# Last two output pairs by token halves, and what follows them: a two-block model kernel on one Trainium2 core

## The reference

```python
y = concat([hyena_out, attn_out]) @ w_out_2          # 2048 x 2048
x = x + rmsnorm(y, post_mix_gain_2)                  # mean square over the 2048 channels of a token
z = rmsnorm(x, pre_ffn_gain_2)
gu = z @ w_up_2                                      # then a 3-tap convolution, gelu(gate) * up
x = x + rmsnorm(h @ w_down_2, post_ffn_gain_2)       # the output
```

## Time and profile before

| | us |
|---|---|
| device time, median of 3 runs | 2695.18 (2695.12 to 2695.7) |
| profiled execution, device time | 2694.55 |
| its span, first to last instruction | 2692.7 |
| PE busy in it | 2670.3 |

### The profile page before, as it was taken

How to read it: one execution, slowest core, us unless ns; L and a number is a source line. 1 busy time by engine, 2 the same in 40 slices (tenths; PEclk the granted TensorE clock), 3 DMA queues, 4 the chain that set the end, 5 groups by cost and what they waited for, 6 DMA issues and landing times.

```text
span 2692.7 us, 40238 instructions
## 1 busy us (share of the span) xinstructions
PE 2670.3 (99%) x14726; PEld 2327.2 (86%) x14726; DVE 1733.7 (64%) x1908; ACT 1279.2 (48%) x1354; POOL 23.0 (1%) x39
## 2 busy tenths in 40 slices
PE   8999999999999999999999999999999999999998
PEld 7888888888888888888888888888888888888887
DVE  7646566667767555555555667778677764577755
ACT  6444444444445444434444555545554443444443
POOL 0000000000011000000000000000000000000000
PEclk9999999999999999999999999999999999999999
DMA  6555455455555555565555555443545555555553
GB/s 237 198 188 172 172 187 180 165 185 188 189 174 198 187 187 198 172 206 191 187 189 171 183 201 173 165 146 130 214 146 190 190 206 196 194 188 187 187 189 139
DMA packets 74948, 494.44 MB, mean 184 GB/s; under 512 B 8711, under 2 KB 9640, under 8 KB 22072
## 3 DMA queue, kind: packets, MB, share of 16 engines
q1 hardware_dynamic: 74728, 493.41, 53.2%
q10 hardware_dynamic: 144, 0.01, 0.0%
HBM read 491.29 MB, written 2.10 MB: 183 GB/s over the span
## 4 chain that ended last, share of the span: by engine, by line
PE 96%; DVE 1%; ACT 1%; issue 1%; DMA 0%; SPq 0%; DVEq 0%; ACTq 0%
PE acc L1851 50%; PE acc L1859 26%; PE acc L1904 7%; PE acc L1910 4%; PE acc L1979 2%; PE acc L1984 1%; ACT w_hi L607 1%; PE acc L2117 1%; PE aux L2199 1%; PE aux L2264 1%; DVE w_lo L1093 0%; DMA raw<-in_w_in 0%; PE aux L2011 0%; PE acc L2124 0%; PE aux L2229 0%
## 5 line engine op out<-in xcount | busy, mean ns | idle before, releaser
L1093 DVE TENSOR_TENSOR w_lo<-raw,w_hi 128x2048 fp32r<-128x2048 f32 (+2 forms) x483 | 1048.8, 2173 | 361.1 <-ACT w_hi L607 315.2
L607 ACT ACTIVATE w_hi<-raw 128x2048 fp32r<-128x2048 f32 (+2 forms) x483 | 879.6, 1821 | 781.4 <-PE acc L1851 500.8
L1851 PE MATMUL acc<-xa,w_hi 128*128 128x512 f32 x5056 | 1212.7, 392 | 0.8 <-ACT w_hi L607 0.6
L1851 PEld LDWEIGHTS acc<-xa,w_hi 128*128 128x128 f32 x5056 | 930.4, 188 | 187.3 <-issue 5.0
L1859 PEld LDWEIGHTS acc<-xa,w_lo 128*128 128x128 f32 x5056 | 648.2, 191 | 24.5
L1859 PE MATMUL acc<-xa,w_lo 128*128 128x256 f32 x5056 | 655.8, 283 | 0.0
L1105 DVE TENSOR_TENSOR tmp<-acc,small 128x512 f32<-128x512 f32 x136 | 94.1, 692 | 297.5 <-ACT small L617 297.3
L1851 PE MATMUL acc<-hid,w_hi 128*128 128x512 f32 x704 | 172.0, 392 | 0.0
L1904 PE MATMUL acc<-w_hi,hid 128*128 128x512 f32 x704 | 167.7, 389 | 0.0
L1904 PEld LDWEIGHTS acc<-w_hi,hid 128*128 128x128 f32 x704 | 132.1, 188 | 27.3
L1851 PEld LDWEIGHTS acc<-hid,w_hi 128*128 128x128 f32 x704 | 128.1, 189 | 23.9
(11 more groups left out here) (326 smaller groups left out, 1610.2 us busy)
## 6 DMA issues: line engine op xcount, KB each, us to landing
raw<-in_w_in SPq DMA_DIRECT2D x158, 1024.0 KB, 4.9
raw<-in_w_gate_up SPq DMA_DIRECT2D x88, 1024.0 KB, 4.9
raw<-in_w_up SPq DMA_DIRECT2D x87, 1024.0 KB, 4.9
raw<-in_w_down SPq DMA_DIRECT2D x64, 704.0 KB, 4.1
raw<-in_w_down SPq DMA_DIRECT2D x40, 1024.0 KB, 4.9
raw<-in_w_out SPq DMA_DIRECT2D x32, 1024.0 KB, 4.9
raw<-in_w_down SPq DMA_DIRECT2D x8, 512.0 KB, 3.6
raw<-in_w_uq SPq DMA_DIRECT2D x3, 1024.0 KB, 4.9
```

Source lines behind the costliest of these rows:

```text
L607: act.activation(hi_part(u, run)[:, 0:kt * P], raw[:, u % RAW, 0:kt * P], ACT.Copy).then_inc(hi_made, splits(u, run))
L1093: dve.tensor_tensor(lo_part(u, run)[:, 0:kt * P], raw[:, u % RAW, 0:kt * P], hi_part(u, run)[:, 0:kt * P], ALU.subtract).then_inc(lo_made, ...
L1851: last = pe.matmul(acc[:, bnk], w_hi[:, u % SPLIT, k * P:(k + 1) * P], x[:, k0 + k], start=first and k == 0, stop=False)
```

## The change

Four things:

- Units 12 and 13 of the output projection are split into `xa` (free at that time) instead of `w_hi`/`w_lo`. The last **two** pairs are then walked by token halves: both pairs for c = 0, then both for c = 1 (before: the last pair alone). The reads of c = 0 (`hyena_branch`, squares, gains, root, residual) move in front of those of c = 1 on DVE and ACT, and the transposes of pieces 0 to 3 stand within the last pairs on PE.
- `first_part(i)` multiplies the low weights with its own piece, 128 columns each, for all eight pieces.
- At the end the sum for the last root (`out_sums(1)`) stands before `finished(3, 0)`.
- The last piece is finished and stored in two halves of 256 channels.

```diff
+        def early_unit(u, run):
+            return isinstance(run, int) and U_LAST <= u + run < U_LAST + 2
...
         def hi_part(u, run):
+            if early_unit(u, run):
+                return place(u + run - U_LAST)
             return next_hi[:, u + run - U_FF2] if next_unit(u, run) else w_hi[:, u % SPLIT]
...
-                if u >= SPLIT:
+                if early_unit(u, run):
+                    act.wait_ge(lo_used, U_WO2)
+                elif u >= SPLIT:
                     act.wait_ge(hi_used, consumed(u, run))
...
+            for n in range(2):
+                late_pair(n, 0).then_inc(half_done, 1)
+            late_pair(0, 1)
+            turn_z(0)
+            turn_z(1)
+            late_pair(1, 1, between=lambda: (turn_z(2), turn_z(3)))
...
-                    if c:
-                        for k in range(4 * g, 4 * g + 4):
-                            last = pe.matmul(dst[:, 1], lo_part(u, 0)[:, k * P:(k + 1) * P], xa[:, k, 0:S], start=False, stop=(k == DT - 1))
+                    for k in range(4 * g, 4 * g + 4):
+                        last = pe.matmul(dst[:, 1, c * P:(c + 1) * P], lo_part(u, 0)[:, k * P:(k + 1) * P], xa[:, k, c * P:(c + 1) * P],
+                                         start=False, stop=(c == 1 and k == DT - 1))
...
             end_gain(1)
+            out_sums(1)
             finished(COLS - 1, 0)
             out_rstd(1)
-            for c in range(COLS):
+            for c in range(COLS - 1):
                 finished(c, 1)
+            for half in range(2):
+                finished(COLS - 1, 1, slice(256 * half, 256 * (half + 1)))
```

More of the change, by code:

```diff
@@ L456, in build_program, with place @@
         LATENTS = ((0, QT), (QT, QT + KVT))
+        MIXED = [(q, c) for q in range(COLS, 2 * COLS - 2) for c in range(2)] + [(q, c) for c in range(2) for q in (2 * COLS - 2, 2 * COLS - 1)]
+        U_LAST = U_WO2 + 2 * (2 * COLS - 2)
+        def early_unit(u, run):
+            return isinstance(run, int) and U_LAST <= u + run < U_LAST + 2
+        def place(n):
+            return xa[:, 4 * n:4 * n + 4].rearrange("p a s -> p (a s)")
         def next_unit(u, run):
@@ L484, in consumed @@
                 return (U_WO2 + 8, U_WO2 + 8, U_FF2 - 1, U_FF2)[u + run - U_FF2]
+            if isinstance(run, int) and U_LAST + 2 <= u + run < U_FF2:
+                return u + run - 3
             return run + (u - 1)
@@ L578, in _ @@
                         unit(u0 + 2 * GT + j, 2 * DOWN * i, d["w_down_2"][g], 2 * DOWN * i + j, 1024 if j % DOWN == DOWN - 1 else 2048)
-            for n in range(2 * COLS):
+            for n in range(2 * COLS - 1):
                 c, g = n // COLS, n % COLS
@@ L582, in _ @@
                 sp.dma_start(out[c, :, g * 512:(g + 1) * 512], h_tok[:, g, c]).then_inc(out_stored, 16)
-            sp.wait_ge(out_stored, 16 * 2 * COLS)
+            for half in range(2):
+                cols = slice(256 * half, 256 * (half + 1))
+                sp.wait_ge(fin_made, 2 * COLS + half)
+                sp.dma_start(out[1, :, D - 512 + 256 * half:D - 256 + 256 * half], h_tok[:, COLS - 1, 1, cols]).then_inc(out_stored, 16)
+            sp.wait_ge(out_stored, 16 * (2 * COLS + 1))
         @block.scalar
@@ L984, in _ @@
             z_high(0)
+            mix_square(6, 1)
+            z_high(1)
+            z_high(2)
+            z_high(3)
             mix_square(7, 1)
-            z_high(1)
             root_of(mix_mean, 2, r_mix[:, 1:2], r_mix[:, 1:2], mix_root)
-            for i in range(2, 6):
-                z_high(i)
+            z_high(4)
+            z_high(5)
             split(U_FF2 + 2)
@@ L1090, in split @@
                 dve.wait_ge(hi_made, made(u, run))
-                if u >= SPLIT:
+                if early_unit(u, run):
+                    dve.wait_ge(lo_used, U_WO2)
+                elif u >= SPLIT:
                     dve.wait_ge(lo_used, consumed(u, run))
@@ L1720, in _ @@
             split(U_WO2 + 15)
[L1721 to L1724, removed]
+            hyena_branch(6, 0)
+            branch_gain(6, 0)
             hyena_branch(7, 0)
@@ L1731, in _ @@
             residual(2)
+            residual(3)
+            hyena_branch(6, 1)
             z_low(0)
+            branch_gain(6, 1)
+            z_low(1)
+            z_low(2)
             hyena_branch(7, 1)
-            residual(3)
+            z_low(3)
             mix_sum(1)
             branch_gain(7, 1)
-            z_low(1)
             mix_rstd(1)
[L1739 to L1743, removed]
+            residual(4)
+            residual(5)
+            z_low(4)
+            residual(6)
+            z_low(5)
+            residual(7)
+            z_low(6)
+            z_low(7)
             split(U_FF2 + 2)
```

52 lines of the change are left out of this document (27 added, 25 removed).

## The result

The changed kernel takes **2700.12 us** (median of 14 runs, 2699.53 to 2703.15) against 2695.07 us (14 runs, 2694.63 to 2696.08): a ratio of 1.0019, 95% interval 1.0012 to 1.0026. The forecast was 2700.2 us in a range of 2697.2 to 2705.6. A second set gave 2700.33 against 2695.16.

A forecast was written before the change was run, and what follows sets the result against it. PE was taken as the bound, busy 2670.3 of 2692.7 us. +5.8 us up to `z_high(7)` and -0.5 at the end gave +5.3, 2699.9 against the profiled execution; median forecast 2700.2 us, range 2697.2 to 2705.6.

The forecast's parts named there:

- A wait that moves forward: Before unit 12: PE now waits there for DVE's reads of pair 5, idle from 1923.79 to 1926.75, +2.96 us.
- the change does what it is arranged for: Rival: no new wait at unit 12, no idle time, no slow clock; sum no change; chance 2 in 100.
- The clock: Behind the wait at unit 12: PE's clock falls to half for a stretch of some 3.4 us, +1.7 us.
- the clock does not fall: Rival: full clock behind the new wait, 1.7 us less, +3.6 us, 2698.5 us; chance 0.18.
- The two pairs and four transposes: Unit 12 to `first_part(0)`: 96 matmuls 21.8 us, transposes 1.7 us; idle times of 0.31 and 1.63 us go.
- The low products: In `first_part`: 64 matmuls of 128 columns at 0.112 us replace 32 of 256 at 0.120, +3.3 us on PE.
- the fp32 rate: Rival: narrow low matmuls take 0.224 us each; +10.4 us, about 2705, or +8.7 without the clock's fall; chance 0.20.
- the cheap ones: Rival: narrow low matmuls take 0.056 to 0.08 us each; +2 to +4.3 us, 2697 to 2699; chance 0.11.
- the 0.62 that the prediction named as a sign: In `first_part`: four low matmuls of 128 columns were to last 3 x 0.112 + 0.28 = 0.62 us.
- Up to `z_high(7)`, and FFN unit 4: `z_high(7)` ends 5.8 us later, at 1966.2 to 1966.4; FFN unit 4 follows at about 1982.65, waiting 1.2 to 1.7.
- one of the prediction's own signs of being wrong: Wrong if `z_high(7)` ends other than about 42.5 us after PE is free for unit 12.
- The end: Last root and piece: earlier sum -0.43 us, halves cost DVE up to 0.15, smaller transfer offsets it; -0.5 us.

The follow-up runs named there:

- experiment 1: Changed kernel with the `acc_free` wait for pair 7 put back before unit 14: 2699.35 us.
- experiment 2: Changed kernel, wait back before unit 14, plus unit 14 split earlier (2700.37 us), unit 15 split earlier (2698.10) or both (2696.68).
- wide_low: Changed kernel with the low products of the first two FFN units again 32 matmuls of 256 columns: 2698.86 us.
- tail_only: Kernel before with only the two end edits, `out_sums(1)` ahead of `finished(3, 0)` and the last piece in halves: 2694.83 us.
- wait_act: Changed kernel, wait back before unit 14 and unit 14 split ahead of pair 5's squares and gains: 2700.37 us.

## Why the prediction came out

**A wait that moves forward, +2.96 us: size right (3.00), only one of two causes.** ACT's two splits in a row, DVE's order, and the end of the reads 0.1 us ahead of PE's start all came as written. But the step takes the place of the wait for the whole cause, and the rival that does without it ("the change does what it is arranged for") misses what is late next. With the wait back in place nearly the same 3 us stand at units 14 and 15 (experiment 1). What costs them there is the walk by halves itself: it wants unit 14 5.4 us earlier than before and unit 15 too, while their splits stand where they stood, unit 15's behind an FFN unit whose raw weights have not landed (experiment 2). The prediction followed pair 5's readers and never asked when PE would next be hungry. That cannot be seen in the time of the changed kernel, where both accounts give the same number; it is luck that the cause left out costs no more than the one that was counted.

**The clock, +1.7 us: wrong in every trace.** The clock stayed at 1.00 behind the 3.0 us in three traces of three (changed kernel twice, wide_low). The rival "the clock does not fall" was the right case there, and 2698.5 was 1.6 us too low for it: the transposes, the end and the base below account for 1.0 of that.

**The two pairs and four transposes: 0.4 us too little.** From unit 12's real start to `first_part(0)` it is 1951.97 - 1928.06 = 23.91 us against 23.5. The rows show half of it: the low products of unit 15 start at 1938.19, 1.87 us after the high ones instead of 1.81, and c = 1 starts 1.04 us after them instead of 0.91; DVE's split of unit 15 ends at 1938.13. So the late unit 15 reaches into the changed kernel too.

**The low products, +3.3 us: right.** From 1952.84 to 1956.52 stand 16 matmuls of 256 and 16 of 128 columns: 3.68 us, 0.115 each; with 0.120 for the wide ones the narrow ones take 0.110 (0.112 forecast). 64 x 0.110 - 32 x 0.120 = +3.2. Both other prices fall, the fp32 rate (0.224) and the cheap ones. Four low matmuls last 0.56 us, not the 0.62 that the prediction named as a sign: the last of them ends sooner than a wide one (0.56 - 3 x 0.110 = 0.23 instead of 0.28). The Trainium skill ("TensorE: Matmul & The Clock Gate", section on the back-to-back issue gap) gives about 81 ns a matmul at 128 columns for a stream of loads and matmuls. The measured 110 ns differs from it and decides. The section on LDWEIGHTS of the same page of the Trainium skill gives 107 ns for a load of 128 columns (128 divided by 1.2 GHz). The measured 110 ns is near to that.

**Up to `z_high(7)`, and FFN unit 4: right without the clock.** `z_high(7)` ends at 1965.26 + 1.14 = 1966.40, 41.34 us after PE was free for unit 12; 42.5 was forecast, and another time than that was one of the prediction's own signs of being wrong. Without the clock it is 40.8, and the 0.5 between are the 0.4 above and short waits. FFN unit 4 starts 16.30 us later (16.35 forecast), its wait is 1.38 us (1.2 to 1.7).

**The end, -0.5 us: mis-sized, -0.2.** The reciprocal did come nearer to PE's last matmul, by 0.42 us (2692.32 against an end at 2689.96; the earlier trace rows has 2686.88 against 2684.10). The halves on DVE cost 0.88 us for 0.75, as allowed for. What was taken as equal was not: the smaller last transfer gives nothing back. From issue to landing, in the last microseconds of the changed kernel's trace (KB each, median us), the two sizes take the same time:

```profile
out<-h_tok SPq DMA_DIRECT2D x5, 256.0 KB, 2.5
out<-h_tok SPq DMA_DIRECT2D x2, 128.0 KB, 2.5
```

**The base.** The trace that the sum was built on had a slow clock in this stretch that the second trace of before and tail_only, the same program up to the end, have not: 52.62 and 52.84 instead of 53.07, 0.3 us more to lose. That is also what the slow clock cost there, where the prediction put 0.9 us.

**From the sum to the median.** The prediction's own sum gives 2700.5, not 2700.2: +5.3 on the profiled execution is 2699.9, and the runs' median lies 0.6 above that execution. The forecast took only half of it, without a reason, and came nearer to the measured 2700.12 by that.

The sum with the measured terms: 4.1 (forecast without the clock) + 0.5 + 0.3 = +4.9 us up to FFN unit 4, -0.2 at the end: +4.7, against +5.05 and +5.17 in the medians. Some 0.4 us are not traced, and the interval of the ratio (1.0012 to 1.0026, so 3.2 to 7.0 us) is wider than that. A slow clock in part of the runs, as in wait_act's trace, would do it, but no row shows it for the changed kernel. There is a hint, no more: take from a median's distance to before what its stretch (over 52.7) and its end (-0.2) explain. In the three sets with the 3.0 us at unit 12 there remain +0.3 to +0.7 us, in the other versions -0.4 to +0.2 (wait_act's with the slow clock of its trace).

## What to carry to other kernels

When a walk is turned so that a result is finished earlier, every input of the turned part is due earlier too: list the due time of each before and after (here unit 15's split, behind another unit's split that waits for its own transfer), and not only the first wait that the code shows. An idle time tells what ended it, not what would stand there next; take the wait away in thought and look where PE would be hungry again. And a stretch between two instructions of the same trace can tell half a microsecond apart, where the 11 or 14 device times of one version here spread over 0.8 to 3.6 us.

## What the runs showed of the hardware

The clock fell in one place where PE was busy, and did not in another where PE was empty. In eleven of thirteen traces the granted clock is at 0.50 (1.2 GHz) for some 3.4 us, from a time between 38.1 and 39.9 us on. It falls within 1.0 us after the end of 3.7 us of matmuls whose stationary and moving tiles fill 16 of 128 rows (the row at 35.17 above; PE busy throughout), and the 16 matmuls behind them take 5.5 us (38.82 above). In the first trace of the kernel before, the same short-row matmuls are followed by no fall, and the 16 take 3.9:

```profile
38.83 3.93 PE L1851 MATMUL acc<-xa,w_hi 128*128 128x512 f32 x16
```

That is 1.6 us, as much as the start of unit 12 differs between the two traces of before (1925.41 - 1923.79 = 1.62). It is not all that moves this start: wait_act, without the slow clock at 39 us, has unit 12 at 1924.22, and tail_only, with it, at 1924.44. The two traces without it (the first of before, and wait_act) are the two that have a slow clock in the stretch of this study: at 1951.58, after PE's 1.63 us of waiting, and in wait_act after 1.95 us:

```profile
1931.90:1934.49 2.59, 0.64 (x3) 0.19 (x2) 1.76 (x1) 2.54 (x2) 0.00 (x0) 1.00 0.59 247
1934.49:1938.95 4.46, 4.46 (x12) 3.33 (x13) 3.60 (x4) 0.72 (x2) 0.00 (x0) 0.62 0.23 31
```

The 3.0 us at unit 12 left it at 1.00 three times. The same 1.63 us of waiting in the kernel before was followed by 0.50 in one trace and not in the other. Which of its waits a program pays for with the clock is thus not fixed by the program; no experiment here separates what decides it.

Narrow fp32r matmuls (128 columns, a new stationary tile each) run at 0.110 us, not at the 0.224 us of two fp32 passes.
